# Two sets of edits in a float32 decoder kernel: weights set aside at three stage ends, and a reordered gated-delta recurrence

## The reference, cut to what matters

```python
for i in range(4):
    h = rms_norm(x, norm_w[i])
    # 0: gated short convolution   1: FoX attention, 8 heads
    # 2: gated delta net (GDN), 8 heads, chunks   3: sliding window attention (SWA) with rope
    x = x + mixer[i](h)
x = rms_norm(x, final_norm_w)
# second block: h = norm(x); stick-breaking attention, mLSTM, cross attention to mem (256 rows)
# y_xa uses _rmsnorm(mem, g_mem) @ w_mem_kv; three gated branches @ w_o; gated feed-forward with convolution
```

```python
decay = where(causal, exp(g_cum[:, None] - g_cum[None, :]), 0)
L = strict(k_beta @ k.T * decay);  T = inverse(eye + L)
u, w = T @ v_beta, T @ (k_beta * exp(g_cum))
# over the chunks
v_new = u_c - w_c @ state
o = q_dec @ state + qk_c @ v_new
state = state * exp(g_last) + k_dec.T @ v_new
# then o * rsqrt(mean(o*o)) * w_onorm * silu(z), and @ w_out
```

## Time and profile before

| | us |
|---|---|
| median of 3 runs | 2245.62 (2243.03 to 2245.72) |
| the profiled execution | 2245.29 |
| its span, first to last instruction | 2243.5 |
| PE busy | 2131.7 (95%), 12942 matmuls |
| DVE busy | 1482.5 (66%) |
| ACT busy | 551.5 (25%) |
| POOL busy | 336.9 (15%) |
| mean granted TensorE clock | 0.982 |

### The profile page before, as it was taken

The page is one execution under the profiler, slowest core; times in us unless marked ns, Lnnn a source line. Parts: engine busy times, 40 slices in busy tenths (PEclk is TensorE's granted clock), DMA queues, the critical chain, the costliest instruction groups (busy, mean ns, idle before and its releaser), DMA issues.

```text
span 2243.5 us, 31830 instructions
## 1 busy us (share of the span) xinstructions
PE 2131.7 (95%) x12942; PEld 1649.2 (74%) x12942; DVE 1482.5 (66%) x2255; ACT 551.5 (25%) x961; POOL 336.9 (15%) x322
## 2 busy tenths in 40 slices
PE   8999999998999999889989999799899999999998
PEld 6888777776767766667777666566678888788786
DVE  6666566666666766487886677444465677958765
ACT  1000222232534444312662133333230011000000
POOL 1111111111000000011101111000111122112111
PEclk9999999999999999989999999899999999999999
DMA  4332222211211111122122221110123332332322
GB/s 164 97 94 95 85 76 76 76 53 52 67 39 49 48 49 39 53 66 75 57 67 66 92 75 59 38 47 29 48 72 98 94 112 85 92 105 85 103 83 87
DMA packets 48977, 165.39 MB, mean 74 GB/s; under 512 B 6336, under 2 KB 6464, under 8 KB 48576
## 3 DMA queue, kind: packets, MB, share of 16 engines
q1 hardware_dynamic: 48544, 162.05, 23.2%
q10 hardware_dynamic: 288, 1.31, 0.2%
HBM read 161.24 MB, written 2.10 MB: 73 GB/s over the span
## 4 chain that ended last, share of the span: by engine, by line
PE 76%; DVE 18%; ACT 2%; issue 2%; DMA 0%; DVEq 0%; POOL 0%; SPq 0%; ACTq 0%
PE ps_lin L1590 19%; PE ps_lin L1592 18%; PE ps_lin L1591 18%; PE ps_att L1636 12%; PE ps_aux L1636 5%; DVE arena L371 4%; DVE w_lo L365 3%; DVE arena L365 3%; ACT arena L1129 2%; DVE arena L368 2%; DVE y_lo L365 1%; PE ps_att L1639 1%; DVE v_tmp L365 1%; PE ps_lin L1607 1%; PE ps_lin L1609 1%
## 5 line engine op out<-in xcount | busy, mean ns | idle before, releaser
L1590 PE MATMUL ps_lin<-xw_hi,w_hi 128*128 128x512 f32 (+1 forms) x1744 | 719.4, 412 | 13.5 <-DVE w_lo L365 11.1
L1592 PE MATMUL ps_lin<-xw_hi,w_lo 128*128 128x512 f32 (+1 forms) x1744 | 684.4, 392 | 0.0
L1591 PE MATMUL ps_lin<-xw_lo,w_hi 128*128 128x512 f32 (+1 forms) x1744 | 683.9, 392 | 0.0
L347 POOL TENSOR_SCALAR w_hi<-raw 128x1024 fp32r<-128x1024 f32 (+4 forms) x317 | 336.5, 1062 | 1891.6 <-PE ps_lin L1592 1752.8
L365 DVE TENSOR_TENSOR w_lo<-raw,w_hi 128x1024 fp32r<-128x1024 f32 (+4 forms) x317 | 378.4, 1194 | 50.5 <-POOL w_hi L347 17.4
L1590 PEld LDWEIGHTS ps_lin<-xw_hi,w_hi 128*128 128x128 f32 (+1 forms) x1744 | 326.1, 187 | 99.3 <-DVE w_lo L365 16.1
L1129 ACT ACTIVATE arena<-arena 128x512 f32<-128x512 f32 (+6 forms) x305 | 191.0, 631 | 814.4 <-DVE arena L371 368.7
L1592 PEld LDWEIGHTS ps_lin<-xw_hi,w_lo 128*128 128x128 f32 (+1 forms) x1744 | 325.6, 187 | 75.1 <-issue 0.3
L1591 PEld LDWEIGHTS ps_lin<-xw_lo,w_hi 128*128 128x128 f32 (+1 forms) x1744 | 326.2, 187 | 73.9 <-issue 9.6
L365 DVE TENSOR_TENSOR arena<-ps_lin,rstd 128x512 f32<-128x512 f32 (+2 forms) x213 | 146.5, 688 | 242.2 <-PE ps_lin L1592 228.9
L1590 PE MATMUL ps_lin<-y_hi,w_hi 128*128 128x512 f32 (+1 forms) x584 | 224.7, 385 | 20.4 <-DVE w_lo L365 15.3
(11 more groups left out here) (155 smaller groups left out, 1749.2 us busy)
## 6 DMA issues: line engine op xcount, KB each, us to landing
raw<-in_w_up SPq DMA_DIRECT2D x44, 512.0 KB, 3.5
raw<-in_conv_w_in SPq DMA_DIRECT2D x32, 512.0 KB, 3.6
raw<-in_fox_w_in SPq DMA_DIRECT2D x32, 512.0 KB, 3.5
raw<-in_gdn_w_in SPq DMA_DIRECT2D x32, 512.0 KB, 3.5
raw<-in_w_gate SPq DMA_DIRECT2D x24, 512.0 KB, 3.5
raw<-in_swa_w_in SPq DMA_DIRECT2D x20, 512.0 KB, 3.5
raw<-in_w_ml SPq DMA_DIRECT2D x16, 512.0 KB, 3.5
raw<-in_w_down SPq DMA_DIRECT2D x16, 512.0 KB, 3.5
```

The lines of the kernel that those rows point to most:

```text
L347: pool.tensor_scalar(w_hi[:, n % SPLIT, 0:kc * c], raw[:, n % RAW, 0:kc * c], 1.0, 0.0, mult, add).then_inc(s("w_rounded"), 1)
L1590: pe.matmul(o, wh, hi, start=first and k == 0, stop=False)
L1591: pe.matmul(o, wh, lo, start=False, stop=False)
L1592: ins = pe.matmul(o, wl, hi, start=False, stop=last and k == kc - 1)
```

## The change

Two sets of edits are joined. Nothing is computed differently but for the order and the engine of some steps.

1. **One unit aside at each of three stage ends.** Unit 3 of `fox_w_out`, `gdn_w_out` and `swa_w_out` (`ASIDE`) is split into arena space that is free by then, through `w_whole` and `w_piece`. POOL waits for a score or inversion count in place of `unit_done`. The subtract stands in the last head (`weights(tile_of("fox_w_out", 1))` and the like). At the stage end the three x additions run first (`together=BANKS`), then the norms with the next two subtracts between.
2. **SWA end on PE.** Slices 0 to 2 of the three tiles come before the turn of head 6, slice 3 between the turn and the pv, 4 and 5 after it, and slice 6 before the last pv, which had stood behind it.
3. **GDN start on DVE.** The first q tile's steps are woven between those of the gate rows.
4. **GDN heads.** exp(g) of the next head is made before the output's square (`gdn_growth`); the gate of head h-1 (`gdn_gate`) stands behind vb of head h; one piece of "A" moves in front of the last chunk's wait; one piece of "tok" moves in front of the k transposes. In the last head, slices 0 and 1 of the three output tiles stand in the places of `LAST_PIECE`.
5. **Angles and memory.** Positions are loaded by SP at the start, the angles made by DVE in conv groups 1 to 6 and cosine and sine by ACT in group 6. The memory's rounding goes to ACT (`mem_hi`) and its squares are summed by PE in eight matmuls.

```diff
-        ARENA = 12560
+        ARENA = 12560 + T
...
-        mem_sq = arena[:, 0:ND * MEM]
+        mem_sq = arena[:, 14 * T:14 * T + ND * MEM]
...
+        ASIDE = {LAST_UNIT[tile_of(w, 3)]: w for w in ("fox_w_out", "gdn_w_out", "swa_w_out")}
...
-        GDN_FILL = {"tok": 4, "squares": 4, "A": 5, "U0": 3}
+        GDN_FILL = {"tok": 4, "squares": 4, "A": 4, "U0": 3}
         LAST_FILL = sum(GDN_FILL.values())
+        LAST_PIECE = {1: (0, 0), 2: (0, 1), 3: (1, 0), 5: (1, 1), 6: (0, 2), 7: (1, 2)}
+        LAST_PIECE.update({LAST_FILL + i: (2 + i // BANKS, i % BANKS) for i in range(12)})
...
+            sp.dma_start(angle["pos"].bitcast(i32), a["positions"]).then_inc(s("pos_in"), 16)
...
-                if n >= SPLIT:
+                if ASIDE.get(n) == "fox_w_out":
+                    pool.wait_ge(s("sm_scores"), NT * (FOX_H - 1))
+                elif ASIDE.get(n) == "gdn_w_out":
+                    pool.wait_ge(s("gdn_T"), 5 * (GDN_H - 2) + 4)
+                elif ASIDE.get(n) == "swa_w_out":
+                    pool.wait_ge(s("sm_scores"), SCORES["swa"] + 4 * (ND - 2))
+                elif n >= SPLIT:
                     pool.wait_ge(s("unit_done"), n - SPLIT + 1)
...
+                if ASIDE.get(n) == "fox_w_out":
+                    dve.wait_ge(s("v_turned"), FOX_H - 1)
+                elif ASIDE.get(n) == "swa_w_out":
+                    dve.wait_ge(s("sm_scores"), SCORES["swa"] + 4 * ND)
...
-            def residual(tiles, norm, beside=None):
-                for m in range(ND):
-                    ps, freed = take(tiles[m])
+            def residual(tiles, norm, beside=None, together=0):
+                def added(m):
+                    ps, freed = take(tiles[m], m >= together)
                     tt(x[:, m, :], x[:, m, :], ps, add).then_inc(s(freed), 1)
                     dve.wait_ge(s(freed), reads(tiles[m]))
+                for m in range(together):
+                    added(m)
+                for m in range(ND):
+                    if m >= together:
+                        added(m)
+                    elif m != 1:
+                        weights(tiles[2 if m == 0 else 3])
                     if norm is not None:
                         normed(m, norm)
...
             for j in range(ND):
+                if j:
+                    next(angles, None)
...
+                if r == FOX_H:
+                    weights(tile_of("fox_w_out", 1))
...
+            first = gdn_tile(0, 0)
...
+            for _ in range(3):
+                next(first)
             dve.wait_ge(s("softplus_out"), 2)
...
+            for _ in range(2):
+                next(first)
             dve.wait_ge(s("gdn_eg"), NT + 1)
...
+            for _ in first:
+                pass
             dve.wait_ge(s("rows_turned"), 1)
...
+                if h:
+                    gdn_gate(h - 1)
                 if h == GDN_H - 1:
                     weights(tile_of("gdn_w_out", 0))
...
+                if h == GDN_H - 1:
+                    weights(tile_of("gdn_w_out", 1))
                 fill(GDN_FILL["U0"])
...
-                        fill(1)
+                    fill(1)
+
+            def gdn_gate(h):
...
-                if m == 0:
-                    dve.wait_ge(s("mem_sq"), 4)
-                    for n in (4, 2, 1):
-                        tt(mem_sq[:, 0:n * MEM], mem_sq[:, 0:n * MEM], mem_sq[:, n * MEM:2 * n * MEM], add).then_inc(s("mem_added"), 1)
-                        dve.wait_ge(s("mem_added"), made("mem_added"))
-                step(ts(memv[0][:, m, :], memx[:, m, :], col("g_mem_2", m), mult))
+                dve.wait_ge(s("mem_hi"), m + 1)
                 stt(memv[1][:, m, :], memx[:, m, :], col("g_mem_2", m), memv[0][:, m, :].bitcast(f32), mult, sub).then_inc(s("mem_ready"), 1)
...
-            residual([tile_of("gdn_w_out", m) for m in range(ND)], 3, beside)
+            residual([tile_of("gdn_w_out", m) for m in range(ND)], 3, mem_normed, BANKS)
...
+                if j == ND - 1:
+                    weights(tile_of("swa_w_out", 0))
                 for half in range(2):
                     swa_masked(j, half)
...
+            def gdn_growth(h):
                 use(ACT.Exp)
                 act.wait_ge(s("gdn_bc"), 2 * h + 1)
                 activation(F["eG"][:, h % 2, :], ps_att[:, 2, :], ACT.Exp).then_inc(s("gdn_bcG"), 1)
...
-                for c in range(NT - 1):
+                for c in range(NT):
                     fill(1)
+                if h < GDN_H - 1:
+                    gdn_growth(h + 1)
                 act.wait_ge(s("gdn_out"), h + 1)
...
+            for m in range(ND):
+                act.activation(memv[0][:, m, :], memx[:, m, :], ACT.Copy, scale=col("g_mem_2", m)).then_inc(s("mem_hi"), 1)
...
+                fill(1)
                 pe.wait_ge(s("gdn_vn_out"), NT * h)
                 pe.wait_ge(s("gdn_qk"), 2 * h + 2)
...
-                fill(GDN_FILL["tok"])
+                fill(GDN_FILL["tok"] - 1)
...
+                    if c == NT - 1:
+                        fill(1)
                     pe.wait_ge(s("gdn_vn_out"), NT * h + c + 1)
...
-                        if r == GDN_H and LAST_FILL <= done[0] < LAST_FILL + 12:
-                            three_one((done[0] - LAST_FILL) // BANKS, (done[0] - LAST_FILL) % BANKS)
+                        if r == GDN_H and done[0] in LAST_PIECE:
+                            three_one(*LAST_PIECE[done[0]])
...
-            three(4, ND)
+            three(6, ND)
...
-            mm(ps_aux[:, 0:MEM], mat("mean_d"), mem_sq[:, 0:MEM]).then_inc(s("mem_ss"), 1)
+            for m in range(ND):
+                last = mm(ps_aux[:, 0:MEM], mat("mean_d"), mem_sq[:, m * MEM:(m + 1) * MEM], m == 0, m == ND - 1)
+            last.then_inc(s("mem_ss"), 1)
...
+                else:
+                    three(0, 3)
                 if j:
                     swa_turn(j - 1, True)
...
+                else:
+                    three(3, 4)
                 if j:
                     swa_pv(j - 1)
-            three(0, 5)
+            three(4, 6)
             swa_turn(ND - 1, False)
-            three(5, 6)
+            three(6, 7)
             swa_pv(ND - 1)
-            three(6, 7)
             three(7, ND)
```

151 lines of the change are left out of this document (88 added, 63 removed).

## The result

| | before | after |
|---|---|---|
| median, us | 2245.67 (4 runs) | 2206.90 (4 runs, 2205.29 to 2214.55) |
| ratio | | 0.9834, 95% interval 0.9808 to 0.986 |
| span of the profiled execution | 2243.5 | 2203.5 |
| PE busy / clock | 2131.7 / 0.982 | 2121.2 / 0.989 |
| PE waits for w_lo, in projection tiles and slices | 26.4 us, 17 times | 16.6 us, 17 times |

The prediction was 2208.0. The stages can be read in both traces by the same instruction, since both kernels run the same matmuls in nearly the same order. The lead of the kernel after at such an anchor is "start before" minus "start after"; the growth of the lead from one anchor to the next is what that part won.

A forecast was written before the change was run, and what follows sets the result against it. TensorE, busy 95% of the span, was taken as the bound. Gains 5.3 + 3.9 + 5.3 - 1.0 + 15.0 + 10.6 = 39.1, less half of 2 x 1.7, gave 37.4 us: 2208.0 us, range 2198 to 2220.

The forecast's parts named there:

- Part 1: FoX end: the fourth unit subtracted early removes a 3.59 us wait and a 1.7 us low-clock restart; gain 5.3 us.
- Rival C: Stage ends: aside units are not ready early, so the fourth-unit waits stay; 2227 us, chance 0.04.
- Part 2: GDN start: weaving the q convolution into the gate rows removes the 4.46 us wait, the first grows 1.5; gain 3.9 us.
- Part 3: GDN heads: thirteen waits of 0.73 us go, new waits of 0.6 us in each of seven heads; net gain 5.3 us.
- rival D: GDN heads: PE's pieces and DVE's chain wait on each other at every level; slower, 2256 us, chance 0.03.
- Part 4: Last GDN head: PE waits some 2.5 us for the third weight unit, inversion starts about 1 us later; -1 us.
- Part 5: GDN end: waits, low clock and moved pieces won, less seven more matmuls (3.15) and a y wait (1.5); gain 15.0 us.
- Part 6: SWA end: slices and the aside unit cover waits of 4.92, 0.82 and 3.60, less 1.9 for y; gain 10.6 us.
- rival A: Behind the three stage ends: DVE does not keep up, POOL's roundings stretch its steps, 6.4 us; 2214 us, chance 0.12.
- The low clock: GDN and SWA ends: two new idle stretches (2.5 and 1.9 us) may bring it; half of 2 x 1.7 us taken off.
- The rule: DVE beside POOL: a two-SBUF-input VectorE step contends with GpSimd reading SBUF; a rounding beside stretches it, 1.94 against 1.23 us.

The follow-up runs named there:

- e1: Changed kernel with the fourth weight unit back in its ordinary slot at the three stage ends, each x addition followed by its norm again: 2219.87 us.
- e2: Changed kernel with exp(g) of each GDN head made right before its decay differences again, not a head ahead: 2212.25 us (one run).
- e4: Changed kernel with the norms of x tiles 4 to 7 at the SWA end moved behind the last sum of squares: 2199.03 us (one run).
- e6: Changed kernel with one convolution step instead of three ahead of softplus and three instead of two ahead of the rows, GDN start: 2204.57 us (one run).
- e11: Changed kernel plus late SWA norms, early third weight unit, other GDN-start weave, seventh SWA slice behind the last pv, memory mean by one matmul: 2195.97 us.
- e13: e11 with the norms of x tiles 4 to 7 late at the GDN end as well, behind the last sum of squares: 2196.67 us.
- e9: Changed kernel with DVE's gate product at the end of each GDN head again, exp(g) still a head ahead: 2212.07 us (one run).
- e3: Changed kernel with the piece ahead of the fourth copy of vn given back to the A group in the GDN heads: 2208.75 us (one run).
- e5: Changed kernel with the third weight unit's subtract in the last head moved ahead of kbg, kd, vb and the gate on DVE: 2207.26 us (one run).
- e10: Changed kernel with the memory's mean by one matmul instead of eight, DVE's three additions behind the fifth norm: 2207.44 us (one run).
- e12: The changed kernel run once more, unedited, on the same chip as e11: 2205.25 us (4 runs).

## Why the prediction came out right

**Part 1** (5.3, measured 6.3) held; e1 takes away 6.2. The kernel before had a low stretch over 472 to 476 us (clock 0.53 and 0.62) that the kernel after has not. It was not counted, and it comes and goes between executions: with nothing edited in FoX the stage takes 284.8 to 284.9 us where the clock is low between 470 and 478 (e2, e4, e6, e11, e13) and 283.9 to 284.0 where it is not. Before and e1 have it too, so without it the gain is 5.3 and e1's loss 5.3 as well. Rival C falls: no aside unit is awaited at any of the three ends.

**Part 2** (3.9, measured 4.5): the second wait went and the first rose by 1.2 where I had 1.5; e6 shows that the rise is the two steps too many ahead of the softplus step.

**Part 3** (5.3, measured 7.6 up to the seventh head) has the step that was most off among those that were worked out. The waits of 0.73 went, and e2 and e9 show that the second of them needed both edits, as stated. But of the 0.6 us of new waits in each head (0.25, 0.2, 0.15) only the first is in the trace: 0.19 before U0. The 0.2 at level 4 and 0.15 at the norm of k were charged to PE although DVE idles 2.6 us per level there, a figure that the prediction itself used against rival D, which falls by the same rows. Over six heads 12 x 0.73 = 8.8 us of wait went and 285.1 - 276.6 = 8.5 us were won. That is more than e3's price of 0.35 per head for the piece leaves room for: e3 itself is 1.0 us per head shorter than the kernel before, with the 0.7 before the v transposes gone, and where its other 0.3 comes from is open.

**Part 4** (-1.0, measured -1.5): the 2.5 us wait for the third unit came as 2.09. The term left out is the wait of 0.98 for the second unit, whose subtract stands behind an evacuation (889.64). e5 wins back 1.5.

**Part 5** (15.0, measured 15.9) held, term by term: no w_lo wait, y wait 1.32 for 1.5, seven more matmuls 3.16 (3.61 x 7 / 8) for 3.15. The claim that DVE's cycle is shorter than PE's was right by little: x additions at 946.71 and 951.65 are 4.94 us apart, I had 4.6. e10 and e13 show how little.

**Part 6** (10.6, measured 6.9) is the miss. The end itself came as worked out, with 2.04 for 1.9. The step that failed is one that isn't in it: part 5 asks whether DVE keeps up behind the end, part 6 does not. The SWA end has a second square addition (0.69), and a cycle of 5.34 us against PE's 5.44 leaves nothing to work off the three additions and norms with which DVE starts behind. In its mechanism that is rival A, to which 0.12 was given, at this one end. By its price (0.71 for a rounding beside a step, 1.42 - 0.69 = 0.73 measured in each of four cycles) it was sized rightly, but it was put on three ends and on three roundings each, while it lasts for the eight tiles of one end. e4 puts the cost of DVE's load there at 4.6 us.

**The low clock.** Of the two new idle stretches neither brought it in the profiled execution (2.04 and 1.32 us, clock 1.00 behind both), in e12 the 2.04 did (0.78 over 1155 to 1160), and the unforeseen one of 2.50 did. Over all traces the half chance was fair for one of the two: behind the 2.04 us the clock was 0.66 in the next 5 us in six of the ten traces that have this wait and 1.00 in four, behind the 1.3 us at the GDN end it was 1.00 in all thirteen. The 1.7 us taken off stand against 0.7 lost in the rest.

**Luck.** The total is nearer to the truth than its terms, and that is luck: part 6 is 3.7 short, and part 3 (2.3 more), part 1 (1.0), part 5 (0.9) and the 1.1 us at the start make up for it.

**The rule.** The sentence of the Trainium skill ("SBUF — State Buffer", section "Who interferes with whom") bears on part 6 more than on the place where it was cited: at the SWA end four cycles in a row show a square addition of 1.42 us beside POOL's rounding (1.27 to 1.56 us, against 1.05 alone). The runs agree with it. A step with one tile as its operand is stretched too: the first step of a norm takes 1.27 us beside a rounding (1162.17) and 0.49 alone. Between 1156 and 1193 us the stretched DVE steps are 4.9 us longer than their likes alone (0.49, 0.78, four times 0.73, 0.72), while DVE is never idle and PE's two waits are 3.6 us. So by estimate DVE would have kept up without the roundings beside it. No run took them away, so what share of the 4.6 us they have is open.

## What to carry to other kernels

When waits at a stage end are taken from the bound engine, work out the cycle of the next engine for the stretch behind that end, with every instruction in it and the stretched ones at their stretched price: here 5.34 us against 5.44 turned 3.7 us of gain into a wait 35 us later. Then ask which of its steps nobody waits for before the next sum, and put those behind it; look up on the bound engine's own queue what it takes first, since the same edit won 4.6 us at one end and nothing at the other. Where a chain is held by two edits, undo each alone: both may carry the full price.

## What the hardware showed that was not expected

- An idle stretch of 1.32 us amid a run of 32 equal 32x32 matmuls of the last head (behind the 29th), with no engine at work, in three of the twelve traces of the study (e5, e9, e13) and not in the first traces of before and after. The low level of the clock follows in two of them: 0.50 over 912 to 915 in e5, and 0.50 over 915 to 930 in e13, where the profiled execution took 2206.04 us and the others of that kernel 2195.3 to 2198.4; in e9 it stays at 1.00 (920 to 923).
- The DMA records of the traces point to the loading of PE's instructions. Shorter stretches of the same look, 0.14 to 0.75 us amid equal 32x32 matmuls, stand in all fourteen traces (in the changed kernel's at 771.42, 817.85 and 864.20: 0.44, 0.49 and 0.39), 35 in all with the three long ones. Each of the 35 ends 2.2 to 2.8 us after a load of 16 KB on the instruction queue began, though in these heads such loads are 3 to 24 us apart; in e5 the load begins at 908.69 and PE goes on at 911.31. They are part of the scatter of the heads. No run changed the number or the order of PE's instructions to test it, so it is not shown.
- The clock fell behind an idle stretch of 1.32 us there and stayed up behind one of 1.32 (933.99) and one of 2.04 us (1153.53) in the profiled execution of the changed kernel. Before the sums of the SWA end it was 0.66 in the 5 us behind 2.50 to 2.52 us in seven traces, and 1.00 behind 2.80 and 2.82 us in e12 and e9. The length of the stretch alone does not tell, and the same program differs from one execution to the next.
- A 512-column addition of DVE takes 0.69 us alone and 1.42 beside POOL's rounding, and a 1024-column subtract 1.72 to 2.07 instead of 1.23. Worked out from the rows of the cycle, the two engines take turns and do not share: POOL's rounding starts at 1177.95 inside DVE's xw_lo step (to 1178.40) and is 0.32 us longer than alone, as if it began at 1178.27; 1.05 us later, at 1179.32, it is done, and DVE's addition, started at 1178.43, ends at 1179.85, as if it had begun at 1179.16. In all four cycles with a rounding there (1167.07, 1172.51, 1177.95, 1183.39) both offsets are the same, 0.13 and 0.15 to 0.16 us ahead of the other's end. So an addition beside a rounding costs what is left of the rounding, and a rounding what is left of the step before it.
